# The prologue of a backbone step: job orders written out, tokens in halves, weight slots freed earlier

## The reference

```python
def ada_mods(cvec, w_ada, b_ada):
    m = jax.nn.silu(cvec) @ w_ada + b_ada        # w_ada: 1024 x 6144, per layer
    return jnp.split(m[:, None, :], 6, axis=-1)  # sh1, sc1, g1, sh2, sc2, g2

h = rms_norm(x, p['norm_w'][li, 0]) * (1 + sc1) + sh1
... h @ w_in_even ...                            # 1024 x 3328, then the mixers
x = x + g1 * y
h = rms_norm(x, p['norm_w'][li, 1]) * (1 + sc2) + sh2
x = x + g2 * sq_relu_mlp(h, p['w_mlp1'][li], p['w_mlp2'][li])
```

## Time and profile before

| | us |
|---|---|
| median of 3 runs | 1062.64 |
| lowest, highest | 1061.22, 1063.09 |
| the profiled execution | 1066.67 |
| its span, first to last instruction | 1064.9 |
| TensorE busy in it | 1024.9 (96%) |
| VectorE, ScalarE, GpSimd busy | 572.7, 486.6, 141.7 |
| mean clock granted to TensorE | 0.992 |

### The profile page before, as it was taken

How to read it: one execution, slowest core, us unless ns; L and a number is a source line. 1 busy time by engine, 2 the same in 40 slices (tenths; PEclk the granted TensorE clock), 3 DMA queues, 4 the chain that set the end, 5 groups by cost and what they waited for, 6 DMA issues and landing times.

```text
span 1064.9 us, 17833 instructions
## 1 busy us (share of the span) xinstructions
PE 1024.9 (96%) x7330; PEld 944.4 (89%) x7330; DVE 572.7 (54%) x907; ACT 486.6 (46%) x859; POOL 141.7 (13%) x168
## 2 busy tenths in 40 slices
PE   5899999999999999999999999998899999999997
PEld 2588887787999999999998998987799999999997
DVE  2464676655654444444456666767554544445352
ACT  4345564656453243342345466667455233253341
POOL 0042220001111010010110233432002011010110
PEclk9999999999999999999999999999899999999999
DMA  8787745744825545445444632223123334334311
GB/s 290 259 270 247 235 159 196 241 160 142 278 80 172 166 137 170 147 159 169 147 149 139 202 109 85 85 80 105 58 101 119 120 118 150 127 100 136 119 41 60
DMA packets 157102, 160.44 MB, mean 151 GB/s; under 512 B 3626, under 2 KB 155716, under 8 KB 157028
## 3 DMA queue, kind: packets, MB, share of 16 engines
q1 hardware_dynamic: 155028, 156.50, 44.7%
q0 software_dynamic: 528, 1.70, 0.5%
q10 hardware_dynamic: 1472, 1.18, 0.3%
HBM read 156.09 MB, written 3.28 MB: 150 GB/s over the span
## 4 chain that ended last, share of the span: by engine, by line
PE 88%; ACT 4%; DVE 4%; issue 2%; POOL 1%; DMA 0%; SPq 0%; DVEq 0%; ACTq 0%
PE G L549 62%; PE G L554 11%; PE OB L571 4%; PE TB L523 3%; ACT wH L994 1%; PE SC L889 1%; DVE wL L1447 1%; PE OB L902 1%; PE SC L590 1%; PE SC L663 1%; PE OB L684 1%; DVE opL L1493 1%; DVE nbuf L1483 1%; PE OB L754 1%; PE SC L639 1%
## 5 line engine op out<-in xcount | busy, mean ns | idle before, releaser
L549 PE MATMUL G<-opH,wH 128*128 128x386 f32 (+1 forms) x768 | 269.4, 351 | 5.1 <-DVE wL L1447 4.1
L994 ACT ACTIVATE wH<-raw 128x2048 fp32r<-128x2048 f32 x97 | 185.2, 1909 | 184.6 <-PE G L549 177.6
L549 PE MATMUL G<-opH,wL 128*128 128x386 f32 (+1 forms) x768 | 261.4, 340 | 0.0
L549 PE MATMUL G<-opL,wH 128*128 128x386 f32 (+1 forms) x768 | 261.2, 340 | 0.0
L1447 DVE TENSOR_TENSOR wL<-raw,wH 128x2048 fp32r<-128x2048 f32 x97 | 224.6, 2315 | 55.7 <-ACT wH L994 55.6
L549 PE MATMUL G<-hidH,wH 128*128 128x384 f32 x512 | 173.3, 338 | 0.0
L549 PE MATMUL G<-hidH,wL 128*128 128x384 f32 x512 | 172.1, 336 | 0.0
L549 PE MATMUL G<-hidL,wH 128*128 128x384 f32 x512 | 172.1, 336 | 0.0
L549 PEld LDWEIGHTS G<-opH,wH 128*128 128x128 f32 x768 | 145.8, 190 | 15.7 <-issue 6.4
L549 PEld LDWEIGHTS G<-opL,wH 128*128 128x128 f32 x768 | 145.7, 190 | 1.4
L549 PEld LDWEIGHTS G<-opH,wL 128*128 128x128 f32 x768 | 145.7, 190 | 0.0
(11 more groups left out here) (239 smaller groups left out, 1182.8 us busy)
## 6 DMA issues: line engine op xcount, KB each, us to landing
raw<-in_w_mlp SPq DMA_DIRECT2D x64, 1024.0 KB, 5.3
raw<-in_w_ada SPq DMA_DIRECT2D x48, 1024.0 KB, 5.8
raw<-in_w_in_even SPq DMA_DIRECT2D x13, 1024.0 KB, 7.0
raw<-in_w_in_odd SPq DMA_DIRECT2D x12, 1024.0 KB, 5.0
raw<-in_w_out_even SPq DMA_DIRECT2D x4, 1024.0 KB, 6.7
raw<-in_w_out_odd SPq DMA_DIRECT2D x4, 1024.0 KB, 5.0
xin<-in_x_sample SPq DMA_DIRECT2D x1, 1024.0 KB, 6.6
out_y_sample<-yout SPq DMA_DIRECT2D x1, 768.0 KB, 4.0
```

What stands on the lines that cost most here:

```text
L549: mm = pe.matmul(G[:, s, 512 * m:512 * m + cols], w[:, s, k, P * m:P * m + P], a[:, k, 0:cols], start=first and q == 0, stop=last and q == 2)
L994: act.activation(wH[:, u % 2, :, :], raw[:, pos % RAW, :, :], ACT.Copy).then_inc(w_high, 1)
```

## The change

- The first jobs of TensorE, ScalarE and VectorE are written out as three lists, `PRO_PE`, `PRO_ACT`, `PRO_DVE`, which a loop on each engine carries out; `psum_uses` reads the order of the buffers from `PRO_PE`.
- The tokens are loaded in two halves of 512 channels, with a semaphore each. The seven vector loads are issued by ScalarE; the vectors of conditions (`v1`) have their own semaphore and are turned behind token tile 1, the others (`v0`: norm weights and adaLN biases) behind `ada4`. Odd token tiles are copied to `xT` by VectorE instead of ScalarE.
- In each adaLN pair the scale piece comes first, in the stream and in the products. VectorE forms the scale as soon as that piece is there; the shift is waited for where it is used.
- Stream: a4, a0, u0, a5, a1, a6, u1, a2, a7, a3, u2, u3, then as before.
- Units 0, 1 and 2 are split in halves of four tiles; TensorE waits for the first half ahead of tile 0 and for the whole ahead of tile 4. ScalarE's and VectorE's lists put the eviction of unit 0 between the halves of unit 2.
- A slot that held an adaLN piece is given back when its product is done (`ob_full`), no longer after ScalarE's copy.
- The four norm rows and the angle table are loaded by GpSimd's queue once the second half of the tokens has landed, on a semaphore of their own; seven tables stay on SP, and their readers wait for those. The block masks are made behind `adt12`.

```diff
-ADA_FIRST = [0, 4, 1, 5, 2, 6, 3, 7]
+ADA_FIRST = [4, 0, 5, 1, 6, 2, 7, 3]
...
-STREAM = [("u", 0), ("a", 0), ("a", 4), ("u", 1)] + [("a", _a) for _a in ADA_FIRST[2:]] + [("u", 2), ("u", 3)]
+STREAM = [("a", 4), ("a", 0), ("u", 0), ("a", 5), ("a", 1), ("a", 6), ("u", 1), ("a", 2), ("a", 7), ("a", 3), ("u", 2), ("u", 3)]
...
+PRO_PE = """
+    x0 x1 v1 x2 x3 x4 x5 x6 x7 ada4 v0 ns5 adt4 ada0 ns6 ns7 adt0 ada5 adt5 ada1 adt1 u0.00 ada6 u0.13 adt6 u1.00 ada2
+    u1.11 adt2 ada7 u1.22 adt7 ada3 u1.33 adt3 u1.44 u0.47 u1.57
+""".split()
+PRO_ACT = """
+    cx0 sq0 cv1 sg sq1 cx2 sq2 lbe cx4 sq3 sq4 cx6 sq5 sq6 ada4 cv0 sp0.0 sq7 sp0.1 ada0 nr ada5 sh0 sh1 ada1 sh2 sh3
+    ada6 sp1.0 sp1.1 ada2 sh4 ada7 sh5 ada3 sh6 sh7
+""".split()
+PRO_DVE = """
+    cx1 cst sum1 lbm cx3 sum2 cx5 sum3 sum4 cx7 sum5 lb adt4 scl0 sp0.0 sp0.1 adt0 sc0 sc1 adt5 scl1 lo0 sc2 adt1 lo1
+    sc3 lo2 lo3 sp1.0 sp1.1 adt6 scl2 sc4 sc5 adt2 lo4 lo5 adt7 scl3 sc6 sc7 adt3 lo6 lo7
+""".split()
...
-                        sp.wait_ge(ob_free, OB_USE[f"ada{n}"] + 1)
+                        sp.wait_ge(ob_full, OB_USE[f"ada{n}"] + 1)
...
+            for half in range(2):
+                cols = slice(D // 2 * half, D // 2 * half + D // 2)
+                sp.dma_start(xin[:, 0, cols], t["x_prompt"][0][:, cols]).then_inc(x_in[half], 16)
+                sp.dma_start(xin[:, 1:3, cols],
+                             t["x_sample"][0].rearrange("(a p) d -> p a d", p=P)[:, :, cols]).then_inc(x_in[half], 16)
...
-                    pe.wait_ge(w_split, u + 1 + 8 * g)
+                    if u < 3:
+                        pe.wait_ge(half_split, u + 1)
+                    else:
+                        pe.wait_ge(w_split, u + 1 + 8 * g)
...
+                    if u < 3 and n == 4:
+                        pe.wait_ge(w_split, u + 1)
...
+            def half_split_high(u, h):
+
+                pos, part = POS["u", u], slice(4 * h, 4 * h + 4)
+                if h == 0:
+                    act.wait_ge(raw_in[pos % RAW], 16 * (pos // RAW + 1))
+                    if u >= 2:
+                        act.wait_ge(gemm_done, u - 1)
+                act.activation(wH[:, u % 2, part, :], raw[:, pos % RAW, part, :], ACT.Copy).then_inc(w_high if h else half_high, 1)
...
+            def half_split_low(u, h):
+
+                pos, part = POS["u", u], slice(4 * h, 4 * h + 4)
+                dve.wait_ge(w_high if h else half_high, u + 1)
+                dve.tensor_tensor(wL[:, u % 2, part, :], raw[:, pos % RAW, part, :], wH[:, u % 2, part, :].bitcast(F32),
+                                  ALU.subtract).then_inc(w_split if h else half_split, 1)
...
+            def pair_scale(j):
+                dve.wait_ge(mods_set, ADA_FIRST.index(4 + j) + 1)
+                dve.wait_ge(tb_free, TB_USE["vecs0"] + 1)
                 sc = mods[:, 0, KT * SC1 + 2 * j:KT * SC1 + 2 * j + 2, :]
                 w = normw[:, 0, 2 * j:2 * j + 2].rearrange("p (t o) -> p t o", o=1).broadcast_to([P, 2, 2])
                 settle(dve.scalar_tensor_tensor(scale1[:, 0, 2 * j:2 * j + 2, :], sc, 1.0, w, ALU.add, ALU.mult))
...
-            pool.wait_ge(even_in, 16 * 12)
+            pool.wait_ge(x_in[1], 32)
+            for n, name in enumerate(("swa_qnorm_w", "swa_knorm_w", "diff_qnorm_w", "diff_knorm_w")):
+                pool.dma_start(wrow[:, n, :], t[name].broadcast_to([P, HD])).then_inc(rope_in, 16)
+            pool.dma_start(trig[:, :, :, :], t["trig"]).then_inc(rope_in, 16)
+            pool.wait_ge(rope_in, 16 * 5)
```

More of the change, by code:

```diff
@@ L166, in psum_uses @@
 def psum_uses():
[L168 to L173, removed]
+    sc, tb, ob = [], [], []
+    for name in PRO_PE:
+        kind, i = job(name)
+        if kind == "x":
+            (sc if i % 2 else tb).append(name)
+        elif kind == "v":
+            tb.append(f"vecs{i}")
+        elif name == "ns5":
+            sc.append("norm0")
+        elif kind == "ada":
+            ob.append(name)
+        elif kind == "adt":
+            tb.append(f"ada{i}")
     for name in EVEN_PE:
@@ L597, in last_norm_sums, with turn_x @@
                     norm_sum(n, k)
[L600 to L607 removed]
+            def turn_x(k):
                 buf, full, out = ("sc", sc_full, SC) if k % 2 else ("tb", tb_full, TB)
+                pe.wait_ge(x_in[2 * k // KT], 32)
                 take(buf, f"x{k}")
@@ L1060, in _ @@
-            act.activation(lb, lb, ACT.Exp).then_inc(cexp_set, 1)
-            act.wait_ge(ones_set, 1)
-            for k in range(KT):
-                buf, free, uses, src = ("sc", sc_free, SC_USE, SC) if k % 2 else ("tb", tb_free, TB_USE, TB)
-                full(buf, f"x{k}")
-                act.activation(xT[:, k, :], src[:, 0:NTOK], ACT.Copy).then_inc(free, 1)
-                act.wait_ge(free, uses[f"x{k}"] + 1)
-                square(0, k)
-                if k == 3:
-                    split(0)
@@ new lines, in _, with copied_x @@
+            act.preload_act_table_set("natural_log_exp_and_others")
+            def copied_x(k):
+                act.wait_ge(*((sc_free, SC_USE[f"x{k}"] + 1) if k % 2 else (tb_free, TB_USE[f"x{k}"] + 1)))
+            for name in PRO_ACT:
+                kind, i = job(name)
+                if kind == "cx":
+                    full("tb", f"x{i}")
+                    act.activation(xT[:, i, :], TB[:, 0:NTOK], ACT.Copy).then_inc(tb_free, 1)
+                elif kind == "sq":
+                    copied_x(i)
+                    square(0, i)
+                elif name == "cv0":
+                    full("tb", "vecs0")
+                    act.activation(vecs[:, 0:P], TB[:, 0:P], ACT.Copy).then_inc(tb_free, 1)
+                elif name == "cv1":
+                    full("tb", "vecs1")
+                    act.activation(vecs[:, P:P + 26], TB[:, 0:26], ACT.Copy).then_inc(tb_free, 1)
+                elif kind == "sg":
+                    act.wait_ge(tb_free, TB_USE["vecs1"] + 1)
+                    act.activation(sgt, vecs[:, P:P + 16], ACT.Exp, scale=-1.0).then_inc(cexp_set, 1)
+                elif kind == "lbe":
+                    act.wait_ge(lbmax_sub, 1)
+                    act.activation(lb, lb, ACT.Exp).then_inc(cexp_set, 1)
+                elif kind == "ada":
+                    ada_copy(i)
+                elif kind == "nr":
+                    act.wait_ge(ones_set, 1)
+                    norm_rstd(0)
+                elif kind == "sh":
+                    shift(0, (i,))
+                elif kind.startswith("sp"):
+                    half_split_high(int(name[2]), int(name[4]))
```

183 lines of the change are left out of this document (87 added, 96 removed).

## The result

The changed kernel takes 1056.12 us (median of 11 runs) where the one before took 1063.09 (11 runs beside them). One run of the changed kernel, 1961.6 us, was disturbed and is left out of the ratio. The ratio is 0.9916, with a 95% interval of 0.9900 to 0.9932: about 8.9 us faster (7.2 to 10.6). It compares the groups of runs and not the two medians, which lie 7.0 us apart. The forecast was 14.7 us faster, 1048; the direction was right, the size was not, and the time lies 2.6 us above the upper end of the range.

A forecast was written before the change was run, and what follows sets the result against it. TensorE and the weight stream were taken to bound the prologue, the only place to win. Unit 2's product at 50.1 us, 15.0 earlier, less 0.3 for block masks, gave 14.7 off 1062.64: 1047.9, say 1048 us; range 1044 to 1053.5.

The forecast's parts named there:

- The change can win only in the prologue, and what it wins there is kept: Before unit 2's product at 65.06 us: gains arise only there and last if the later stage stays bound by TensorE.
- a floor of 48.0: End of the prologue: earliest start of unit 2's product, from the tail at 47.0 us and ada 8's product of 1.00.
- the forecast of 50.1: Start of unit 2's product: 48.0 us, plus 1.8 for a low-clock stretch and 0.3 for handovers; 15.0 earlier than 65.06.
- the tail: End of the prologue: after ada 3 lands at 36.2, TensorE has its product, nine tiles, one small turn: 10.8 us.
- The rope tables' five loads on GpSimd's queue: 0 to 0.5, under the same cover: Prologue, under the wait for unit 0: norm-row and angle-table loads cost 0 to 0.5 us, adding nothing to the sum.
- slack of 2.4 us: Weight stream in the prologue: every load is issued at least 2.4 us before its limit, so the stream holds.
- rival (a): Prologue stream breaks at a unit, most likely unit 0; two breaks of 2.5 us, 9.7 gained, 1053 us; chance 0.18.
- one such stretch, +1.8: Prologue: idle pieces between 17 and 25 us bring TensorE one low-clock stretch, adding 1.8 us.
- the 6 us that the prediction gave as a sign of being wrong: TensorE's clock: the prediction counts as wrong if the clock is 0.5 for over 6 us.
- Rival (b): TensorE falls to the low clock two more times, 2 x 1.8 us, giving 1051.6 us; chance 0.10.
- exists because a slot is given back at the product: Weight slots in the prologue: release at the product, not after ScalarE's copy, gives the slack of 2.4 us or more.
- the start at 5.8 us: Start of the prologue: first token turn moves from 11.10 to about 5.8 us, bounds 4.8 and 8.3.

The follow-up runs named there:

- x4: Changed kernel with the five rope-table loads moved from GpSimd to SP, all tables behind piece 9, second run: 1051.34 us, ratio 0.9866.
- e5: Changed kernel with the five rope-table loads moved from GpSimd to SP, all tables behind piece 9, first run: 1050.23 us, ratio 0.9863.
- x1: Changed kernel with GpSimd's four row loads reading 128 different prompt rows instead of one row 128 times: 1051.04 us, one run.
- x3: The changed kernel repeated without any edit: 1055.22 us, ratio 0.9900 to the kernel before.
- e2: Changed kernel with unit 0's split moved behind the last square and norm factor (ScalarE) and the first two scaled tiles (VectorE): 1056.06 us, ratio 0.9924.
- e3: Changed kernel with 17 unneeded identity turns filling TensorE's wait ahead of the last sum of squares: 1053.86 us, ratio 0.9902.
- e7: Changed kernel with adaLN slots given back after ScalarE's copy again: 1054.37 us, ratio 0.9910.
- e11: Kernel with all tables issued by SP behind piece 9, with adaLN slots given back after ScalarE's copy again: 1051.18 us, ratio 0.9883.
- e9: Kernel with all tables issued by SP behind piece 9, with the tokens loaded in two whole transfers: 1050.10 us, ratio 0.9873.
- e1: Changed kernel with GpSimd waiting for unit 0's split before its five rope-table loads: 1055.97 us, ratio 0.9921.
- x2: Changed kernel with the four repeated rows issued by ScalarE behind its seven vector loads, angle table still on GpSimd: 1054.13 us, one run.

## Why the prediction was right in direction and wrong in size

**Right.** "The change can win only in the prologue, and what it wins there is kept": 999.8 against 998.8 us of rest. The rule that TensorE and the stream bound the prologue together: with the five loads away, unit 2 comes at 49.2 to 49.5, beside a floor of 48.0. That this is near the forecast of 50.1 is in part luck: the forecast holds 1.8 us for a low stretch that these profiles do not have. Two more terms came out, the tail (10.8 us foreseen; in the changed kernel the product of piece 3 begins at 42.00 and that of piece 8, behind it all, at 53.13, which is 11.1, with 0.07 us of idle time from 44.00 on) and the split of unit 2, which no longer stands bare. The block masks cost nothing in the later stage, where 0.3 was taken: TensorE is busy for 94.94 of 94.94 us there as before.

**Wrong: the step "The rope tables' five loads on GpSimd's queue: 0 to 0.5, under the same cover".** I priced them by what they issue and carry, 256 KB. Without them unit 0 landed at 17.0 (x4) and 17.9 (e5), where 17.3 was forecast; with 128 different rows at 18.2 (x1); as changed at 20.3, and at 21.3 in x3. So by x1, a single run, the bytes cost up to 1.2 us and the repeated rows 2 to 3 more; of these, the missing 0.38 MB in 4 us (0.93 against 1.31 MB) is 1.0 us at the full rate, and where the rest was lost the queues' totals don't show. Together this is more than the slack of 2.4 us that I had counted for the first units, and it made rival (a), the break at unit 0, come true by a mechanism that I had not listed. I had looked for the break in the order of ScalarE's list, and e2 shows that reordering it gains nothing. In unit 2's product this step is 3.8 us with the clock kept up (e3 against x4), and 4.1 to 5.0 with the low clock that came with it.

**The clock term, "one such stretch, +1.8": not the miss, but not independent.** The low clock lasted some 9.8 us in the prologue (a mean of 0.91 over 54.20 us), over the 6 us that the prediction gave as a sign of being wrong. The idle time of 3.79 us before the last square went with a long low stretch in which TensorE was busy for 8.39 us; kept away by the filler (e3), it turned out to be worth 1.3 us, where I took 1.8. In e5 and x4, without the dip, there was no low stretch. In x1, also without the dip, there was one (0.57 over 20 to 24 us, after an idle wait of 2.10 us), so the dip is not its only cause. Rival (b) and rival (a) had mostly one cause here, and I gave them separate chances.

**Wrong in the conversion to a time.** The gain between the two profiled executions is 1066.67 - 1055.19 = 11.5 us; between the runs it is 8.9. I took a shift read from one of the slower executions off a median that stood 4.0 us lower. So the 14.7 - 8.9 = 5.8 us of the miss are 3.2 in the profile (14.7 - 11.5: the product 4.1 us later than foreseen, the rest of the span shorter by 1.0 where 0.3 more was taken, and 0.4 between span and execution) and 2.6 by this choice. Of the 2.6, 1.0 is the low stretch 700 us on that differs between the two profiles; the rest is inside the interval of the gain.

**Credited wrongly, without effect.** The slack "exists because a slot is given back at the product": it doesn't hang on that (e7, e11). I had misread the row: the 10.9 us of idle time in front of ScalarE's eight copies ended with TensorE's product (`<-PE OB L571 10.9` in the earlier trace rows), so ScalarE waited for the product and the slots did not wait for ScalarE. Nor is the start at 5.8 us needed (it came at 7.00, and e9 with an even later one, 7.88, is as fast). As for the port that VectorE and GpSimd share: GpSimd's tables (20.18 to 21.88 us) overlapped the first low half of unit 0's split for 0.39 us, and it took 1.47 us where the other half took 1.21 and x4's took 1.23. That is +0.25 us; the row's ratio (3.02 / 2.30) gives 0.1. The Trainium skill, SBUF — State Buffer, on the shared port pair, states a lock for the whole instruction; by it the overlap would cost up to 0.39. This run decides for neither, and either is too small to matter. On the clock, the full one (1.00) was granted from the first instruction to 20 us through all the early idle time, and e5 kept it to the end of the prologue. The Trainium skill, TensorE: Matmul & The Clock Gate, part 1, has the throttled state as the default; the trace disagrees here too.

## What to carry to other kernels

A load that repeats one row of memory over all partitions can cost far more than its bytes: in a saturated stream price it by a run of its own, or put it where nothing waits for the stream; delaying it only hands the loss to the next transfer. When idle time and the low clock are both terms of a sum, ask first whether one late transfer would cause both, and do not add them: an engine that works slower may only fill its idle time. And before a shift read in one profile is taken off a median, compare the profiled execution's clock with those of the runs, and look for low stretches far from the change.

## What the runs showed of the hardware

- Four loads of one 256-byte row to 128 partitions each (128 KB in all), issued by GpSimd, held the transfers at 206 to 289 GB/s for 3 to 4 us (after, e1), where 384 to 388 were moved without them; the same loads with 128 different rows left it at 388 (x1). Issued by ScalarE they went with 245 GB/s for 4 us (x2), with the DMA engines 0.80 busy.
- Tokens in four transfers of half rows, beside ScalarE's small loads, slowed the first microseconds: 289 GB/s at 4 to 8 us (e5) against 381 with whole rows (e9).
- The runs of one kernel spread by 0.8% (1061.0 to 1069.4 us for before) with a mean granted clock of 0.996 to 0.988. Around the same idle wait of 3.35 us the granted clock had a mean over 12 us of 0.86, 0.72 or 1.00 (18 profiles).
- A low stretch costs less than its length suggests where the engine would have idled: the changed kernel's prologue had some 9.8 us of it (a mean of 0.91 over 54.20 us) and e3's none, and unit 2 came 1.3 us earlier there, 0.3 against the repeat x3.
